# A planned order of work: ScalarE may stay idle for a piece that is nearly ready, and VectorE takes a first token tile's norms and gating ahead

## The reference, cut to what matters

```python
mixed = concatenate([mix, mo], -1) @ w_out[i]
x = layer_norm(ALPHA * x + mixed, ln1_g[i], ln1_b[i])
x = layer_norm(ALPHA * x + swiglu(x, w_gate_up[i], w_down[i]), ln2_g[i], ln2_b[i])
```

```python
h = rms_norm(x, norm_pre[l]);  u = h @ w_in[l]          # 13 slices of u
y = gates_0 * (oa @ w_br_a) + gates_1 * (ob @ w_br_b) + gates_2 * (oc @ w_br_c)
x = x + rms_norm(y @ w_out[l], norm_post[l])
x = x + sigmoid(x @ w_ple_gate[l]) * (p[l] @ w_ple_proj[l])
```

## Time and profile before

| what | value |
|---|---|
| median of 3 runs | 1910.88 us (1909.26 to 1911.4) |
| the profiled execution's own time | 1908.38 us |
| its span, first to last instruction | 1906.5 us |
| busy: PE, PEld, POOL, ACT, DVE | 98%, 80%, 80%, 50%, 42% of the span |
| granted TensorE clock over the span | 0.998 of full speed |
| read from memory | 325 MB, 172 GB/s over the span |
| matmuls | 9610 |
| splits (line 1213) | 624, 991 ns each in the mean |

### The profile page before, as it was taken

The page is one execution under the profiler, slowest core; times in us unless marked ns, Lnnn a source line. Parts: engine busy times, 40 slices in busy tenths (PEclk is TensorE's granted clock), DMA queues, the critical chain, the costliest instruction groups (busy, mean ns, idle before and its releaser), DMA issues.

```text
span 1906.5 us, 27403 instructions
## 1 busy us (share of the span) xinstructions
PE 1865.8 (98%) x9610; PEld 1529.7 (80%) x9610; DVE 798.1 (42%) x1933; ACT 945.2 (50%) x1501; POOL 1516.2 (80%) x1330
## 2 busy tenths in 40 slices
PE   8999999999999999999999999999999999999999
PEld 7878888877888887788887778887887887788877
DVE  6774110456111245411056641106857344455534
ACT  4564444454444445444435544434656654555743
POOL 7768979885897977797987779797686887777785
PEclk9999999999999999999999999999999999999999
DMA  8445656555666554465655456655564564556453
GB/s 292 137 146 178 187 164 223 179 176 145 184 193 214 188 172 149 144 188 164 223 150 157 152 166 187 208 169 174 178 182 122 161 209 152 162 170 178 130 173 111
DMA packets 184558, 330.54 MB, mean 173 GB/s; under 512 B 12221, under 2 KB 44521, under 8 KB 184425
## 3 DMA queue, kind: packets, MB, share of 16 engines
q1 hardware_dynamic: 176512, 323.21, 55.0%
q10 hardware_dynamic: 7912, 5.59, 1.0%
HBM read 325.35 MB, written 3.41 MB: 172 GB/s over the span
## 4 chain that ended last, share of the span: by engine, by line
PE 84%; POOL 6%; DVE 4%; DMA 3%; ACT 2%; issue 1%; SPq 0%; DVEq 0%; ACTq 0%
PE acc L1419 24%; PE acc L1420 23%; PE acc L1426 21%; POOL w_lo L1185 6%; PE tps L1366 4%; PE acc L1441 2%; PE acc L1422 2%; PE ops L1483 2%; PE tps L1459 2%; DMA raw<-in_w_down 1%; PE acc L1390 1%; PE acc L1392 1%; PE acc L1391 1%; DMA raw<-in_w_mem_kv 1%; PE ops L1378 1%
## 5 line engine op out<-in xcount | busy, mean ns | idle before, releaser
L1185 POOL TENSOR_TENSOR w_lo<-raw,w_hi 128x512 fp32r<-128x512 f32 (+2 forms) x1242 | 1475.3, 1225 | 349.9 <-ACT w_hi L1213 348.7
L1213 ACT CAST w_hi<-raw 128x1024 fp32r<-128x1024 f32 (+3 forms) x624 | 615.6, 991 | 745.3 <-PE acc L1426 567.2
L1419 PE MATMUL acc<-w_hi,xT_hi 128*128 128x512 f32 (+1 forms) x1808 | 687.1, 384 | 4.9 <-ACT U L1247 2.9
L1420 PE MATMUL acc<-w_lo,xT_hi 128*128 128x512 f32 (+1 forms) x1808 | 666.6, 372 | 0.0
L1426 PE MATMUL acc<-w_hi,xT_lo 128*128 128x512 f32 (+2 forms) x1744 | 505.2, 371 | 0.0
L1419 PEld LDWEIGHTS acc<-w_hi,xT_hi 128*128 128x128 f32 x1808 | 341.4, 189 | 74.6 <-issue 15.2
L1420 PEld LDWEIGHTS acc<-w_lo,xT_hi 128*128 128x128 f32 x1808 | 342.2, 189 | 52.4
L1426 PEld LDWEIGHTS acc<-w_hi,xT_lo 128*128 128x128 f32 x1744 | 317.8, 189 | 58.2 <-DVE xT_lo L1696 1.1
L1756 DVE TENSOR_TENSOR H<-G,acc 128x512 f32<-128x512 f32 (+1 forms) x48 | 30.9, 643 | 335.5 <-PE acc L1426 335.5
L1419 PE MATMUL acc<-w_hi,hT_hi 128*128 128x512 f32 x352 | 139.5, 396 | 3.6 <-POOL w_lo L1185 3.4
L1420 PE MATMUL acc<-w_lo,hT_hi 128*128 128x512 f32 x352 | 137.2, 390 | 0.0
(11 more groups left out here) (210 smaller groups left out, 1993.5 us busy)
## 6 DMA issues: line engine op xcount, KB each, us to landing
raw<-in_w_gate_up SPq DMA_DIRECT2D x160, 512.0 KB, 3.9
raw<-in_w_in SPq DMA_DIRECT2D x104, 512.0 KB, 3.8
raw<-in_w_down SPq DMA_DIRECT2D x88, 512.0 KB, 3.7
raw<-in_w_out SPq DMA_DIRECT2D x48, 512.0 KB, 3.6
raw<-in_w_in_a SPq DMA_DIRECT2D x32, 512.0 KB, 3.6
raw<-in_w_in_b SPq DMA_DIRECT2D x20, 512.0 KB, 3.7
raw<-in_w_mem_kv SPq DMA_DIRECT2D x16, 512.0 KB, 4.2
raw<-in_w_gate_up SPq DMA_DIRECT2D x32, 256.0 KB, 2.8
```

Source lines behind the costliest of these rows:

```text
L1185: ins = nc.gpsimd.tensor_tensor(w_lo[:, r, i, 0:ch.width], raw[:, r, i, 0:ch.width], w_hi[:, slot, i, 0:ch.width].bitcast(F32), ALU.subtract)
L1213: nc.scalar.copy(w_hi[:, u.u % SPLIT, 0:u.nk, 0:u.chunk.width], raw[:, u.u % RAW, 0:u.nk, 0:u.chunk.width]).then_inc(S["hi_ready"], 1)
L1419: nc.tensor.matmul(o, hi[:, tok], wh, start=first_k, stop=False)
L1420: ins = nc.tensor.matmul(o, hi[:, tok], wl, start=False, stop=False)
```

## The change

Tasks get an attribute `ahead`: 600 ns for every ACT task that is not a split, 1500 ns for the tasks of `ple_add`, `layer_norm` and `rms_post` (and the scales of the last two) if they belong to t0, and 0 for all others. When `arrange` has chosen a task without `ahead`, it looks at the tasks of the same engine whose predecessors are all placed. If one that has `ahead` (and needs no bank of its own) can start less than min(ahead, cost of the chosen task) after the chosen one would, that one is placed instead, and the engine stays idle until it starts. No instruction is added or removed.

```diff
+LEADS = ("ple_add", "layer_norm", "rms_post")
...
         self.prio = prio
+        self.ahead = 600 if eng == "ACT" and kind != "split" else 0
...
             assert first is not None, [(k.kind, k.it) for t in ready.values() for k in t][:8]
+            k = first[1]
+            if not k.ahead:
+                for other in ready[k.eng]:
+                    at = max(other.at, clock[k.eng])
+                    if other.ahead and other.room is None and at < first[0][0] + min(other.ahead, k.cost):
+                        first = ((at,), other)
+                        break
             k = first[1]
...
-        return self.task("DVE", "stage", Stage(fn, fed, **kw), cost, "stage", fed, prio=prio)
+        one = self.task("DVE", "stage", Stage(fn, fed, **kw), cost, "stage", fed, prio=prio)
+        if fn in LEADS and kw.get("t") == 0:
+            one.ahead = 1500
+        return one
...
             first = p.task("DVE", "stage", Stage(fn + "_scale", fed[t], **st), scale, None, [*fed[t], *taken], prio=t - 1 if fn == "rms_pre" else 0)
+            if fn in LEADS and t == 0:
+                first.ahead = 1500
```

## The result

The changed kernel takes 1914.21 us in the median of 15 runs (1912.51 to 1915.67), the kernel before, run beside it, 1910.76 (1908.77 to 1913.17): ratio 1.0019, 95% interval 1.0012 to 1.0025, or 3.6 us slower. Forecast were 1905.0 us and a range up to 1911.5. In what follows "x us faster" is the ratio's distance from 1 times the median of the kernel before in the same runs; an interval of ±0.0009, as most have, is ±1.7 us, and the difference of two kernels that were each timed against the kernel before is uncertain by some 2.4.

The account below looks back on a forecast made before the run. PE multiplies nearly all the time (1865.8 of 1906.5 us), so order can win only in 40.7 us of idle and lowered clock. 0.98 + 1.16 + 0.3 + 2.2 + 1.3 = 5.9 us off 1910.9 gives 1905.0; range 1899.5 to 1911.5.

Parts of the forecast that it names:

- part 4: Other ACT waits, some 50 in the lists: later splits are hidden by the lead; taken as 0, bound +2 us.
- Part 1: First norms, t0's scale ahead of t1's eviction on DVE: gains 0.98 (layer 3), 1.16 (layer 2), 0.3 us (layer 1).
- Part 2: Entrance of second stack's second layer: t0's sigmoid and add go sooner, PE's idle 2.62 falls to 1.13; gain 2.2 us.
- Part 3: Layer 3's attention: exponentials ahead of a split, PE's 0.93 us wait for a bank goes; gain 1.3 us (0 to 2.5).
- The rule against the change: Second-stack `mix_maps` runs beside POOL's moved subtractions: each caught costs 2.1 us, each freed returns it; taken as 0.
- Slower: Rival: caught `mix_maps` runs in second-stack differential attention stall PE and lower the clock, 3.8 us together; chance 0.09.
- given back: Rival: places gain, but one or two `mix_maps` runs are caught or the entrance's sigmoid isn't moved; 1907 to 1909, chance 0.17.
- place 2: Entrance of the second stack's second layer, the place of Part 2: gain 2.2 us, between 0.6 and 2.6.
- Doesn't do what it says: Rival: planner's clock isn't the chip's, so only Part 1 remains, 2.4 us gained, 1908.5; chance 0.09.
- more: Rival: the other layers' attention chains shorten too, gain 9 us or more, 1901; chance 0.09.
- The sign that was named for a wrong forecast: More PE waits for POOL's `w_lo` or line 2012 than 4.9 and 4.2, a longer cast wait, or new half-clock spell.
- A new spell at half clock: One of the signs named for a wrong forecast; at the entrance of Part 2 the existing spell was to go.

Follow-up runs that it names:

- e13: Kernel before with one decision: in layer 0's attention ACT does step 3's exponentials ahead of the split of unit 41; 1910.5 us, ratio 1.0001.
- e18: Whole change, but only a split ready for less than 1 us by the planner's clock may be passed; 1907.4 us, ratio 0.9988 against the kernel before.
- e11: Kernel before, but in layer 3's attention ACT may wait for exponentials; 1909.6 us, ratio 0.9998.
- e6: Kernel before, but in layer 0 (attention and the norm behind it) the planner may use both new rules; 1912.9 us, ratio 1.0012.
- e7: Kernel before, but both rules allowed in the two stretches with the sink attention and the plain attention ahead of it; 1913.2 us, ratio 1.0015.
- e12: As e7, but in each sink stage the fourth step's exponentials go back ahead of the silu eviction; 1911.4 us, ratio 1.0005 against the kernel before.
- e17: Whole change, but a split may be passed by a waited-for piece once at most; 1909.4 us, ratio 0.9999 against the kernel before.
- the control: The kernel before once more, same lists on every engine, timed beside the kernel before; 1909.5 us, ratio 0.9996.
- e1: The change with its DVE part only (t0's norms and gating go ahead), ACT never waits; 1913.1 us, ratio 1.0017 against the kernel before.
- e8: Kernel before with one ACT exchange: one step's exponentials ahead of a split in the second stack's first differential attention; 1911.7 us, ratio 1.0004.

## Why the prediction was wrong, point by point

*The step that failed* is in part 4: "the split starts later by at most 0.6 plus the other's time", and "What hides it is the lead of up to eight units", with "I take 0 and keep +2 as bound". The second half is right for one decision (e13, ratio 1.0001), and even for a split that is 10 or 11 us late (e18, e11). The first is wrong: the rule looks only at the present choice, so the same split is passed again and again, 16 us in layer 0 (unit 41), 13.8 in layer 3 (unit 363), 16.5 and 16.6 ahead of the sinks (units 490, 584); of the last three, 3 to 5 are the lateness of the whole kernel there. The one in layer 3 cost nothing. Layer 0 cost 2.3 us by e6 (2.5 in the trace of the change), the sinks 2.9 by e7 (3.2 in its trace, 1.4 of it by table loads), against a bound of 2 for all: the lead hides lateness until it is used up. I had treated each of some 50 patterns as an exchange in a list that stays as it is; the planner makes a new list behind every exchange.

*A term that was missing*: ACT's table loads. An eviction and exponentials that change places cost 1.28 us more on ACT. The page of before has 41 loads, and the planner's costs have none; I read past them. 1.9 us by e12 in the times, 1.4 in the traces, and nothing in e17 and e18, where the splits behind them are less late.

*Part 1* holds in the trace: 1.32 us at layers 2 and 3, against 2.48 and 2.30. Three of its claims don't hold. "At layer 0 PE does not wait, gain 0" supposed that layer 0's list stays; there the norm now comes late. The 0.3 forecast for layer 1 isn't there: the transposes do go ahead of t1's last unit, but once both tiles are through, PE is no earlier against the control than it was. And the gain was put to DVE's order alone, while e1 shows that the cast must go ahead of the split as well.

*Part 2* holds in the profile (idle 1.27 for a forecast 1.13, clock kept), except that the low part of x is not there in time: 0.71 us of waiting. In the medians it can't be told from nothing; in the traces it is 2.2, as forecast, against the profile that the forecast was read from, and 1.6 to 1.8 against the control, where this entry in the waits, 5.2 us in the earlier trace rows, is 4.5. In the changed kernel 0.7 of it goes again with the new spell of low clock at 1660 us.

*Part 3*: 1.3 forecast, 0.4 measured (-1.3 to 2.1), 0.6 in the trace. The wait of 0.93 for the bank is gone as forecast; others behind it took part of the gain.

*The rule against the change* was given zero in the sum, as gains and losses in equal number. In number that came out: of the eight runs one was caught (0.75 to 2.33 us at 1345) and one freed (1.58 to 0.75 at 1341), four are long as before. In price it didn't. PE had not waited for the one that was freed, and it does wait for the one that was caught (waits 4.2 to 6.0). This cost 1.8 us in the trace, 0.8 by e8's times, where the forecast had "I take 0": a second step that failed, though its price for a caught run, 2.1, was about right.

*The rivals.* "Slower" had 0.09. Its sign was right, but what came, 3.6 us slower, is less than the 3.8 that the prediction wanted for a difference, and lies in the gap between "given back", which ended at a gain of 1.7, and "slower", which began at a loss of 3.9 (two caught runs, 7.6, against a gain of 3.7 without place 2). The range, up to 1911.5, left out both this gap and "slower". The rival's place (the differential attention) bore the smallest of the three prices, and its threshold of three caught runs wasn't what decided. "Doesn't do what it says" and "more" fell. The sign that was named for a wrong forecast, more waits for `w_lo` or line 2012 than 4.9 and 4.2, came true (8.2 and 6.0), but the control shows that 6.3 for `w_lo` would have meant nothing. "A new spell at half clock" came true as well (1660 us).

## What to carry to other kernels

A look-ahead rule in a greedy planner needs a memory. "Stay idle for a piece that is nearly ready" is cheap once and dear when the same long task is passed until its lead is used up: 16 us in layer 0 cost 2.5, 10 us for one split alone cost next to nothing. A bound on the age of what is passed turned 3.6 us slower into 2.3 us faster with one condition. To price a scheduling rule, keep the old order outside a chosen place, and price place by place: whole plans differ far from where the rule acted. Read the price of a place from when PE is done with each unit in two traces, too: where medians were uncertain by 1.7 us, this told 0.6 from 1.8. And give function-table loads a cost in the plan, or keep exponentials on one side of an eviction.

## What the runs showed of the hardware that was not expected

Two profiles of the same lists differ by 1.4 us in the waits for POOL (4.9 and 6.3) and by 0.9 in those for the memory's keys (1.6 and 2.5), with medians 0.4 us apart (ratio 0.9996); single waits of the kind that this forecast was a sum of are no steadier than that. The idle time of 1.83 us in e8 was followed by a stretch at clock 0.59, and one of 1.80 us in the changed kernel by none (1.00 from 1348 to 1352 us); the idle time of 1.68 us in the second layer's differential attention was followed by 0.72 over 6 us in the changed kernel and by 1.00 in the kernel before. So an idle stretch of this length can go either way, and a forecast can't take a lowered clock, or its absence, from one trace.
